# A ring of six slots for the modulation weights in place of four

## The reference

```python
cond = jax.nn.silu(c)
for l in range(DEPTH):                                   # DEPTH = 2
    mod = cond @ w_mod[l] + b_mod[l]                     # (1, 1024) @ (1024, 9216)
    sh1, sc1, g1, sh2, sc2, g2, sh3, sc3, g3 = jnp.split(mod, 9, axis=-1)
    h = modulate(x, norm_g[l, 0], sh1, sc1)
    x = x + 0.5 * g1[:, None, :] * swiglu(h, w_ffn1_gu[l], w_ffn1_down[l])   # width 2816
    h = modulate(x, norm_g[l, 1], sh2, sc2)
    ...                                                  # three kinds of attention
    x = x + g2[:, None, :] * (mix @ w_out[l])
    h = modulate(x, norm_g[l, 2], sh3, sc3)
    x = x + 0.5 * g3[:, None, :] * swiglu(h, w_ffn2_gu[l], w_ffn2_down[l])
```

## Time and profile before

| | |
|---|---|
| time, median of 3 runs (lowest to highest) | 1846.24 us (1843.24 to 1847.56) |
| the profiled execution: its own time, its span | 1844.28 us, 1842.5 us |
| busy: PE, DVE, ACT, POOL | 97%, 73%, 50%, 9% |
| granted TensorE clock, mean over the span | 0.995 |
| DMA | 439.49 MB, mean 239 GB/s |
| chain that ended last, by engine | PE 76%, DVE 10%, DMA 8%, ACT 3%, issue 2% |
| loads of modulation units by POOL: number, issue to landing | 224, median 6.7 us (`w_mod`) and 6.6 us (`w_ada`) |

### The profile page before, as it was taken

The page is one execution under the profiler, slowest core; times in us unless marked ns, Lnnn a source line. Parts: engine busy times, 40 slices in busy tenths (PEclk is TensorE's granted clock), DMA queues, the critical chain, the costliest instruction groups (busy, mean ns, idle before and its releaser), DMA issues.

```text
span 1842.5 us, 24266 instructions
## 1 busy us (share of the span) xinstructions
PE 1789.8 (97%) x9140; PEld 1456.1 (79%) x9140; DVE 1341.6 (73%) x1825; ACT 919.6 (50%) x1504; POOL 174.4 (9%) x359
## 2 busy tenths in 40 slices
PE   6999999999999999999999999999999999999998
PEld 3877779788877887887888788877778788878886
DVE  6887777787878778777788866477777766577455
ACT  4343467743455434777344644446343644454344
POOL 3011110111101110111111000001111000000000
PEclk8999999999999999999999999999999999999999
DMA  8989842498969796425899555457898554557652
GB/s 324 325 289 352 296 153 102 160 322 297 330 205 328 281 360 232 150 93 183 320 328 322 189 206 181 170 178 264 314 332 320 203 189 139 187 179 243 217 189 85
DMA packets 241444, 439.49 MB, mean 239 GB/s; under 512 B 15200, under 2 KB 157360, under 8 KB 241200
## 3 DMA queue, kind: packets, MB, share of 16 engines
q1 hardware_dynamic: 206608, 311.78, 50.0%
q0 software_dynamic: 34016, 122.74, 17.4%
q10 hardware_dynamic: 704, 3.42, 0.5%
HBM read 436.80 MB, written 1.09 MB: 238 GB/s over the span
## 4 chain that ended last, share of the span: by engine, by line
PE 76%; DVE 10%; DMA 8%; ACT 3%; issue 2%; SPq 0%; POOL 0%; DVEq 0%; ACTq 0%
PE bank L1826 23%; PE bank L1828 22%; PE bank L1827 22%; DVE weights_lo L1152 5%; DMA arena<-in_w_mod 2%; DMA weights_raw<-in_w_ffn_in 2%; DMA arena<-in_w_ada 1%; PE bank L2017 1%; DVE mod_acc L1173 1%; DMA weights_raw<-in_w_mod 1%; ACT weights_hi L693 1%; DVE x L1305 1%; DVE arena L1299 1%; ACT arena L734 1%; PE bank L2211 1%
## 5 line engine op out<-in xcount | busy, mean ns | idle before, releaser
L1152 DVE TENSOR_TENSOR weights_lo<-weights_raw,weights_hi 128x1024 fp32r<-128x1024 f32 (+2 forms) x584 | 671.6, 1200 | 127.5 <-ACT weights_hi L693 126.3
L1826 PE MATMUL bank<-weights_hi,hT_hi 128*128 128x512 f32 (+2 forms) x1696 | 670.0, 395 | 10.7 <-DVE hT_lo L1269 8.8
L1828 PE MATMUL bank<-weights_hi,hT_lo 128*128 128x512 f32 (+2 forms) x1696 | 658.3, 388 | 0.0
L1827 PE MATMUL bank<-weights_lo,hT_hi 128*128 128x512 f32 (+2 forms) x1696 | 657.1, 387 | 0.0
L693 ACT ACTIVATE weights_hi<-weights_raw 128x1024 fp32r<-128x1024 f32 (+2 forms) x584 | 567.7, 1038 | 83.0 <-PE bank L1828 27.8
L1826 PEld LDWEIGHTS bank<-weights_hi,hT_hi 128*128 128x128 f32 x1696 | 318.5, 188 | 78.0 <-issue 7.4
L1828 PEld LDWEIGHTS bank<-weights_hi,hT_lo 128*128 128x128 f32 x1696 | 318.3, 188 | 65.3
L1827 PEld LDWEIGHTS bank<-weights_lo,hT_hi 128*128 128x128 f32 x1696 | 318.9, 188 | 59.6
L869 ACT ACTIVATE actT_hi<-bank 128x512 fp32r<-128x512 f32 x66 | 39.5, 599 | 483.9 <-PE bank L2017 483.9
L1173 DVE SCALAR_TENSOR_TENSOR mod_acc<-arena,silu_cond,mod_acc 128x1024 f32<-128x1024 f32 x184 | 236.2, 1284 | 47.1 <-DMA arena<-in_w_ada 17.0
L1826 PE MATMUL bank<-weights_hi,actT_hi 128*128 128x512 f32 (+1 forms) x616 | 243.7, 396 | 2.8 <-DVE weights_lo L1152 2.7
(11 more groups left out here) (279 smaller groups left out, 1219.3 us busy)
## 6 DMA issues: line engine op xcount, KB each, us to landing
weights_raw<-in_w_ffn_gu SPq DMA_DIRECT2D x176, 512.0 KB, 5.7
arena<-in_w_mod POOLq DMA_DIRECT2D x128, 512.0 KB, 6.7
weights_raw<-in_w_in SPq DMA_DIRECT2D x104, 512.0 KB, 4.8
arena<-in_w_ada POOLq DMA_DIRECT2D x96, 512.0 KB, 6.6
weights_raw<-in_w_ffn_down SPq DMA_DIRECT2D x88, 512.0 KB, 5.0
weights_raw<-in_w_ffn_in SPq DMA_DIRECT2D x88, 512.0 KB, 5.9
weights_raw<-in_w_ffn_out SPq DMA_DIRECT2D x44, 512.0 KB, 4.8
weights_raw<-in_w_out SPq DMA_DIRECT2D x32, 512.0 KB, 4.4
```

The costliest lines, as they stand in the source:

```text
L1152: V.tensor_tensor(wlo[:, n % PARTS, 0:width], raw[:, n % RING, 0:width], whi[:, n % PARTS, 0:width].bitcast(F32), ALU.subtract).then_inc(S ...
L1826: T.matmul(o, sh, wh, start=start, stop=False)
L1827: T.matmul(o, sh, wl, start=False, stop=False)
L1828: return T.matmul(o, sl, wh, start=False, stop=stop)
```

## The change

The ring has six slots. The two more lie at offset 2304 of the arena's first part (`A_T`, `A_S`), which attention and retention use for their scores and turned heads, and the FFNs only below offset 2304. The units ahead of FFN 0 keep a ring of four (`FIRST_RING`). The two semaphores `mod_masked` and `mod_reduced` are gone: `mod_store` waits on the engine's step semaphore in their place, at the same points.

```diff
-MOD_RING = 4
+MOD_RING = 6
+FIRST_RING = 4
...
-        modw = ar(A_MOD, MOD_RING * D).rearrange("p (r n) -> p r n", r=MOD_RING)
+        modw = [ar(A_MOD + D * i, D) for i in range(4)] + [ar(A_T + 2304 + D * i, D) for i in range(2)]
...
-            if m < MOD_FIRST_UNITS and first_home(m) >= MOD_RING:
-                return raw[:, first_home(m) - MOD_RING, :]
-            return modw[:, (first_home(m) if m < MOD_FIRST_UNITS else m) % MOD_RING, :]
+            if m >= MOD_FIRST_UNITS:
+                return modw[m % MOD_RING]
+            return modw[first_home(m)] if first_home(m) < FIRST_RING else raw[:, first_home(m) - FIRST_RING, :]
...
-                w, acc = modw[:, m % MOD_RING, :], modacc[:, chunk % 2, :]
+                w, acc = modw[m % MOD_RING], modacc[:, chunk % 2, :]
...
-                V.tensor_tensor(modm[:, :, :], bank[sum_bank(chunk)][:, 0:256].rearrange("p (k j) -> p k j", k=8), eye, ALU.mult).then_inc(S("mod_masked"), 1)
-                dve.wait_ge(S("mod_masked"), chunk + 1)
-                V.tensor_reduce(modr[:, :], modm[:, :, :], AX, ALU.add).then_inc(S("mod_reduced"), 1)
-                dve.wait_ge(S("mod_reduced"), chunk + 1)
+                then(V.tensor_tensor(modm[:, :, :], bank[sum_bank(chunk)][:, 0:256].rearrange("p (k j) -> p k j", k=8), eye, ALU.mult))
+                then(V.tensor_reduce(modr[:, :], modm[:, :, :], AX, ALU.add))
```

More of the change, by code:

```diff
@@ L434, in first_home @@
         def first_home(m):
-            return m if m < MOD_RING + RING else (m - RING) % MOD_RING if m < 2 * MOD_RING + RING else m - RING
+            return m if m < FIRST_RING + RING else (m - RING) % FIRST_RING if m < 2 * FIRST_RING + RING else m - RING
         def mod_tile(m):
-            if m < MOD_FIRST_UNITS and first_home(m) >= MOD_RING:
-                return raw[:, first_home(m) - MOD_RING, :]
-            return modw[:, (first_home(m) if m < MOD_FIRST_UNITS else m) % MOD_RING, :]
+            if m >= MOD_FIRST_UNITS:
+                return modw[m % MOD_RING]
+            return modw[first_home(m)] if first_home(m) < FIRST_RING else raw[:, first_home(m) - FIRST_RING, :]
         def mod_sem(m):
@@ L1888, in mod_sum @@
                     at = (8 if chunk >= 18 else 0) + 7
-                    terms.append((silc[:, at:at + 1].broadcast_to([P, 32]), modw[:, m % MOD_RING, :]))
+                    terms.append((silc[:, at:at + 1].broadcast_to([P, 32]), modw[m % MOD_RING]))
                 for j, (col, src) in enumerate(terms):
```

## The result

| | before | after |
|---|---|---|
| time, median of 4 runs each (lowest to highest) | 1844.75 us (1843.24 to 1847.56) | 1830.30 us (1829.83 to 1831.42) |
| the profiled execution, its span | 1844.28, 1842.5 us | 1829.83, 1828.0 us |

The ratio is 0.9918, with a 95% interval of 0.9903 to 0.9932. The six-slot ring is faster by 14.4 us. The forecast had the sign, the two places and 9.7 us.

The account below looks back on a forecast made before the run. PE sets the pace and stops behind the modulation ring in FFNs 0 and 4. Terms -7.01 - 3.01 + 0.3 = -9.7 us gave 1834.6, or 1836.5 from the median; forecast 1835.5 us, range 1832 to 1838.5 (8 in 10: 1831.5 to 1841).

Parts of the forecast that it names:

- the place and the mechanism: FFNs 0 and 4: bursts over five or six slots wait on themselves in a four-slot ring; PE lost 7.01 and 5.23 us.
- rival A: FFN 4: DVE waits for ACT and ACT for weights instead; 1840.5 us with half the gain lost (0.07), 1845 with all (0.07).
- B: Start of all six FFNs: first strips' weights come 2.6 us late without PE cover, giving 1851 us; chance 0.04.
- D: FFN 0: the fourth unit behind PE's still lands late, 1 us in three of six blocks, giving 1838.5 us; chance 0.10.
- the rest of the chain stands: FFN 4, unit 206 behind the gate's broadcast: two fewer loads save only 1.04 us, so 2.22 us of PE's loss stays.
- Rival C: FFN 4: unit 206 is not late after all, so all of the 2.22 us comes back, giving 1833 us; chance 0.08.
- the length without a stop: Turn to turn, FFN 4 would need 167.83 us and FFN 0 168.69 us if PE never stopped.
- The first burst: FFN 0's start: two more loads compete with SP's weights; cost between nothing and 2.6 us, taken as 0.3 us.
- the half microsecond that I had allowed: Profile after: the first block of FFN 0 stays within 0.5 us of 17.65 us.
- the whole one that I had named as a sign of being wrong: The first block of an FFN growing by over a microsecond would show the prediction wrong.

Follow-up runs that it names:

- run 1: Changed kernel with six slots, but every load waits for the unit four before it, not six: 1845.61 us, ratio 0.9999 to the kernel before.
- run 2: Changed kernel with the old wait of four slots in FFN 0 only: 1838.11 us, ratio 0.9964 to the kernel before.
- run 3: Changed kernel with the old wait of four slots in FFN 4 only: 1836.49 us, ratio 0.9955 to the kernel before.
- run 4: Changed kernel with units 203 and 204 also waiting for PE's block 4 sum, so three loads lie ahead of FFN 4's gate write: 1833.24 us, one execution.
- run 6: Changed kernel with the six loads at the start of FFN 0 held back until DVE is done with the first strips' weights: 1829.87 us, one execution.
- ring6_again: The changed kernel measured again without any edit: 1830.27 us, ratio 0.9923 to the kernel before.
- run 5: Changed kernel with FFN 4's gate write and broadcast two loads later, so unit 206 is loaded ahead of them: 1830.73 us, ratio 0.9918 to the kernel before.
- run 10: Kernel before (four slots) with 28 matmuls of zeros keeping PE busy ahead of the last turn of FFNs 0 and 4: 1844.59 us, one execution.
- run 8: Changed kernel with FFN 0's first six loads held back and FFN 4's gate broadcast two loads later: 1829.11 us, ratio 0.9916 to the kernel before.
- run 7: Changed kernel with a ring of five slots in place of six: 1833.78 us, ratio 0.9937 to the kernel before.

## Why the prediction was right or wrong

**Right: the place and the mechanism.** All of the gain is in the waits of the loads (run 1), in FFNs 0 and 4 (runs 2 and 3). FFN 0's stops are gone from its turns, FFN 4's too but for one wait of DVE, which is the one for unit 206. FFNs 1 to 3 did not move. Rivals A, B and D did not come. DVE's waits for ACT's rounding did rise in FFN 0, from 5.0 to 12.2 us, but those for the ring fell by 23.6 and the turns drew closer (FFN 4: 11.6 to 12.7 us), and no fourth unit was late (DVE waited 1.0 us in all of FFN 0).

**Wrong, the largest part (2.0 us): "the rest of the chain stands".** I took 1.04 us off unit 206's chain, for two issues, and left 2.22 us of PE's loss in place. Only 0.23 us stayed. FFN 4 gave 5.38 us back and not 3.01; 0.37 of the difference is the length without a stop, below. Rival C, to which I gave 0.08, comes nearest. The working was sound in its form. In all runs in which unit 206 stands behind the broadcast and the clock did not fall in these blocks, what blocks 4 and 5 lose together over 2 x 18.05 us follows from when unit 206 is used, counted from PE's sum of block 4:

| run | loads ahead | write waited for | 206 issued | 206 used | lost by PE | used - lost |
|---|---|---|---|---|---|---|
| before | 3 | 7.14 | 11.15 | 19.20 | 3.26 | 15.94 |
| wait4 | 3 | 6.74 | 11.27 | 19.10 | 3.14 | 15.96 |
| three_ahead | 3 | 7.86 | 12.13 | 18.55 | 2.62 | 15.93 |
| wait4_in_ffn0 | 1 | 6.12 | 9.10 | 16.50 | 0.54 | 15.96 |
| hold_six | 1 | 5.93 | 8.91 | 16.26 | 0.29 | 15.97 |
| ring6_again | 1 | 5.90 | 8.88 | 16.19 | 0.21 | 15.98 |
| after | 1 | 6.00 | 8.98 | 16.17 | 0.23 | 15.94 |

The last column is constant to 0.05 us: PE has cover up to 15.95 us after its sum and pays one for one beyond. So the stop of block 4 and that of block 5 are one, as I had argued. What I mis-sized is the chain. The landings in it are not of fixed length. In FFN 4 the gate's write was waited for 5.9 to 6.1 us in the four executions with one load ahead, 7.70 in the one with two, and 6.6 to 8.3 us in six of the seven with three (6.60 in run 3, 8.31 in run 5). The seventh is run 10, at 5.02 us, below all those with one:

```profile
1329.49 0.55 POOL L583 DMA_DIRECT2D gate_bcast<-gate_scratch  x1 [5.02 <-DMA gate_scratch<-gate_rows]
```

The shortening was 3.03 us and not 1.04, and took away nearly all of the 3.26. That the loads ahead lengthen the write's wait is supported by run 4, which put back only these loads' place. It is one execution, and run 10 says that something else moves the wait by as much. What that is stays open. That unit 206 itself took 0.86 us less from issue to use is measured and its cause is open too: in run 4 it was shorter still (6.42 us).

**Wrong, by omission (1.3 us): what PE loses after it has stopped.** I read PE's loss between turns and so ended the account at the last turn. Behind the stop of 3.24 us came 3.4 us at half clock, and a tail that was 1.33 us longer. Run 10 shows, in one execution, that it is the clock. Run 2 had nearly the same stop and lost 2.4 us in the tail, and in the nine profiles without the stop the tail is 3.80 to 3.86 us. The sign of it was in the trace before: FFN 0's tail was 5.13 us and FFN 1's 3.86.

**Wrong in size: the length without a stop (0.7 us).** I built 167.83 and 168.69 us from the cost of six eight-matmul sums in full. Runs 5, 6 and 8 have 167.46 and 168.34 us. The sixth sum stands in the last block, which takes 9.89 us with it and 9.83 in FFN 1 with a four-matmul sum. So PE had lost 5.60 and 7.36 us before, not 5.23 and 7.01.

**The first burst (0.3 us forecast).** The first block of FFN 0 grew by 1.22 us, past the half microsecond that I had allowed and past the whole one that I had named as a sign of being wrong. The kernel is faster all the same. In the other four profiles with six loads it grew by 0.05 to 1.23 us. The term was too small in this profile by 0.9 us. But the block's end depends on the start as well. It came at 74.70, 75.48, 75.70 and 75.51 us in the runs with four loads there (mean 75.35), and at 75.40, 75.20, 75.64, 76.02 and 75.70 with six (mean 75.59). By the block's end the size of the term is within that scatter. Held back, the block ends at 74.69 (run 6) and at 74.39 (`best`). FFN 0's gain from turn to turn was 6.16 us, where 6.71 was forecast: 7.36 - 1.22 and not 7.01 - 0.3. The two errors hid each other in part, which is luck.

**The rest.** 6.16 + 1.33 + 5.38 = 12.9 of the 14.5 us. Another 0.5 is an earlier first turn (56.53 and 57.05). It lies at 57.05 to 58.04 in the runs with four loads in the first burst and at 56.53 to 57.81 with six; the two overlap. About 1.0 lies in the phases around FFN 4, where the stretch before its first turn took 0.6 us less and the one after it 0.4. The first of these took 227.40 to 228.07 us in the eleven other runs, with 227.49 to 227.65 in the three that have the old wait in FFN 4, where the profile of before has 228.18, the longest of all. The second varies by 0.4 (run 1, whose stretch has a fall of the clock in it, left out). So the first 0.6 us comes from a profile of before that was slow there, the second 0.4 lies within the scatter, and no run shows a part of the ring in either. The interval of the ratio reaches from 12.5 to 17.9 us and can't tell 12.9 from 14.5. The reruns of the changed kernel (1830.27) say that the gain as a whole is not luck.

One slip of the working matters little: rival A reckons with "4.2 us less", where the sum gives FFN 4 3.01 us. That would be 304 and not 305 GB/s.

## What to carry to other kernels

Compare the slots of a ring with the longest burst that reads it. Where the ring is shorter, the reader waits in mid burst for a load that could only start in that burst, and an idle buffer of another phase can give the missing slots. How many are needed depends on the reader's lead: here five slots for bursts of six were enough for PE in FFN 0 (169.44 us, run 7), though DVE still waited. When a queue is shortened, don't hold the landings behind it constant: give them a range. Here one small write was waited for between 5.0 and 8.3 us. And follow a stop of PE past its end in the granted clock, since here the seven stops of 2.26 to 3.29 us that I read were all followed by a few us at 1.2 GHz, which the busy share does not show. Take the length of a stretch without a stop from an undisturbed stretch where there is one, and not from sums of parts.

## What the runs showed of the hardware

- The clock fell to the lower level behind stops of 3.24 us (before), 3.25 (run 1), 3.29 (run 2), 2.96 (run 1, FFN 4) and 2.45 us (run 1, FFN 0), but not behind the 2.18 us of before's FFN 4, whose tail was 3.86 us. It did fall behind 2.26 us in run 10 and 2.31 us in run 3, and behind 1.18 and 0.71 us in run 7, but not behind 1.91 us in run 10 or 1.81 and 0.71 us in run 4. So the length of the stop alone doesn't decide.
- A fall costs PE 1.3 us (tail 5.13 and 3.80) to 2.4 us (6.21). In run 7 block 5 lost 3.55 us, of which unit 206 explains 17.92 - 15.95 = 1.97. I put the other 1.6 to the clock, which was at 0.65 and 0.92 in the two windows of 4 us behind the stops.
- A write of 4 KB in FFN 4 was waited for 5.9 to 6.1 us behind one load of 512 KB on the same queue, and 5.0 to 8.3 us behind three.
- Two more loads of 512 KB on POOL's queue lengthened ACT's waits for SP's weights at the start of FFN 0: 1.3 to 2.4 us in the four profiles with four loads there, 3.6 to 6.4 us in the five with six, none in the two in which the loads were held back (runs 6 and 8).
